# Adaptive weights accumulated in two 128x1024 operations per load in place of four of 128x512

## What is computed

```
cond = jax.nn.silu(c)
for i in range(DEPTH):
    mod = (cond @ ada_w[i] + ada_b[i])[:, None, :]
    sh1, sc1, gt1, sh2, sc2, gt2 = jnp.split(mod, N_MOD, axis=-1)
    h = rms_norm(x, norm1_w[i]) * (1 + sc1) + sh1
    ...                                   # the mixer gives y
    x = x + (1 + gt1) * y
    h = rms_norm(x, norm2_w[i]) * (1 + sc2) + sh2
    x = x + (1 + gt2) * swiglu_ffn(h, ffn_w1[i], ffn_w3[i], ffn_w2[i])
```

## Time and profile before

| | before |
|---|---|
| device time, three runs | 2332.69, 2333.07, 2337.92 us; median 2333.07 |
| profiled execution, its own time | 2324.39 us |
| its span (first to last instruction) | 2322.7 us |
| VectorE busy | 1470.6 us (63%) |
| of it adaptive operations (line 892) | 270.7 us, 384 operations |
| TensorE busy | 1992.9 us (86%) |
| ScalarE busy | 887.3 us (38%) |
| device memory read | 343.93 MB |

### The profile page before, as it was taken

One profiled execution on the slowest core, in us unless ns is written; L12 is line 12 of the kernel. 1 busy time (PEld: TensorE's weight loads), 2 busy tenths in 40 slices (PEclk: granted clock), 3 DMA queues, 4 the chain that ended last, 5 costly groups with the idle time before them and its releaser, 6 DMA issues.

```text
span 2322.7 us, 32348 instructions
## 1 busy us (share of the span) xinstructions
PE 1992.9 (86%) x13189; PEld 1746.3 (75%) x13189; DVE 1470.6 (63%) x2054; ACT 887.3 (38%) x1293; POOL 38.1 (2%) x61
## 2 busy tenths in 40 slices
PE   0597998699979988888898899996889888997998
PEld 0586786688758788883897689666887787886996
DVE  0599588688663666624788623346886497574553
ACT  1243753344332211102444434533443344664552
POOL 3000000100000000000000000001000000000000
PEclk9998999799979999959899889667999699998999
DMA  2554078399704200002698623024888152153562
GB/s 85 178 154 137 32 252 282 121 310 310 265 12 152 84 1 1 1 1 91 218 317 311 224 62 124 15 73 149 304 298 291 30 163 91 55 176 115 183 200 108
DMA packets 221029, 347.08 MB, mean 149 GB/s; under 512 B 12561, under 2 KB 178017, under 8 KB 220881
## 3 DMA queue, kind: packets, MB, share of 16 engines
q1 hardware_dynamic: 215024, 344.22, 44.5%
q10 hardware_dynamic: 5600, 0.36, 0.2%
q0 software_dynamic: 256, 0.43, 0.1%
HBM read 343.93 MB, written 1.05 MB: 149 GB/s over the span
## 4 chain that ended last, share of the span: by engine, by line
PE 48%; DVE 27%; DMA 12%; ACT 8%; issue 4%; ACTq 1%; DVEq 0%
PE psum_dve L353 19%; PE psum_act L353 16%; PE psum_acc L353 11%; DMA ring<-in_ffn_w_dram 9%; DVE arena L892 5%; DVE w_lo L922 5%; DVE arena L1039 4%; ACT w_hi L1348 3%; DMA dskip<-in_m_D_dram 2%; DVE arena L1036 1%; DVE arena L1232 1%; DVE arena L1202 1%; ACT arena L1420 1%; PE psum_act L356 1%; DVE arena L962 1%
## 5 line engine op out<-in xcount | busy, mean ns | idle before, releaser
L922 DVE TENSOR_TENSOR w_lo<-ring,w_hi 128x1024 fp32r<-128x1024 f32 x424 | 508.4, 1223 | 250.3 <-ACT w_hi L1348 247.5
L1348 ACT ACTIVATE w_hi<-ring 128x1024 fp32r<-128x1024 f32 x424 | 450.5, 1062 | 498.4 <-DMA ring<-in_ffn_w_dram 296.7
L353 PE MATMUL psum_dve<-h_lo,w_hi 128*128 128x256 f32 x1216 | 341.3, 281 | 0.0
L353 PE MATMUL psum_act<-h_lo,w_hi 128*128 128x256 f32 x1088 | 308.5, 284 | 0.0
L892 DVE SCALAR_TENSOR_TENSOR arena<-ring,vcol,arena 128x512 f32<-128x512 f32 x384 | 270.7, 748 | 11.1 <-DMA ring<-in_ada_w_dram 7.4
L353 PE MATMUL psum_dve<-arena 128*128 128x128 f32 (+5 forms) x1760 | 228.4, 318 | 16.0 <-DVE arena L1261 4.7
L353 PE MATMUL psum_act<-h_hi_ffn,w_hi 128*128 128x256 f32 x704 | 202.6, 288 | 35.4 <-DVE w_lo L922 18.3
L353 PEld LDWEIGHTS psum_dve<-h_lo,w_hi 128*128 128x128 f32 x1216 | 230.6, 190 | 0.0
L353 PEld LDWEIGHTS psum_dve<-arena 128*128 128x128 f32 (+3 forms) x1760 | 183.7, 193 | 46.3 <-issue 17.0
L353 PE MATMUL psum_dve<-h_hi_ffn,w_hi 128*128 128x256 f32 x704 | 198.0, 281 | 13.8 <-DVE w_lo L922 13.7
L353 PEld LDWEIGHTS psum_act<-h_lo,w_hi 128*128 128x128 f32 x1088 | 209.7, 193 | 0.1
(11 more groups left out here) (249 smaller groups left out, 3431.0 us busy)
## 6 DMA issues: line engine op xcount, KB each, us to landing
ring<-in_ffn_w_dram SPq DMA_DIRECT2D x132, 1024.0 KB, 5.5
ring<-in_ada_w_dram SPq DMA_DIRECT2D x96, 1024.0 KB, 5.4
ring<-in_m_in_w_dram SPq DMA_DIRECT2D x48, 1024.0 KB, 5.4
ring<-in_m_out_w_dram SPq DMA_DIRECT2D x16, 1024.0 KB, 5.6
ring<-in_r_w_rkv_dram SPq DMA_DIRECT2D x12, 1024.0 KB, 5.1
ring<-in_f_qkvf_w_dram SPq DMA_DIRECT2D x12, 1024.0 KB, 5.3
ring<-in_r_out_w_dram SPq DMA_DIRECT2D x4, 1024.0 KB, 4.9
ring<-in_f_out_w_dram SPq DMA_DIRECT2D x4, 1024.0 KB, 4.8
```

The costliest lines, as they stand in the source:

```text
L353: return nc.tensor.matmul(o, l, r, start=start, stop=stop, skip_group_check=True)
L922: tell(V.tensor_tensor(o, raw, hi, ALU.subtract), split_ready, hold=False)
L1348: tell(A(o, raw, ACT.Copy), hi_ready)
```

## The change

Each adaptive load is accumulated by two operations of 128x1024 (k = 0, then k = 1) instead of four of 128x512. The arithmetic for each element and its order (k = 0, then k = 1) stay as they were. The wait for the previous adaptive load's last operation moves from behind the first operation to ahead of it. The first operation is now held (VectorE waits for its completion, since the second adds to all that it wrote), the second is not, and releases the slot as before. No instruction changes its place with regard to others; loads, transfers and the other engines' instructions are the same.

```
-                for k in range(2):
-                    for hf in range(2):
-                        if (k, hf) == (0, 1) and counts.get("ada_slot_used"):
-                            dve.wait_ge(ada_used, counts["ada_slot_used"])
-                        o = ada[:, m * D + hf * NB:m * D + (hf + 1) * NB]
-                        ins = V.scalar_tensor_tensor(out=o, in0=slot(n)[:, k * D + hf * NB:k * D + (hf + 1) * NB],
-                                                     scalar=col("c", 2 * k4 + k), in1=o, op0=ALU.mult, op1=ALU.add)
-                        if k == 1 and hf == 1:
-                            tell(ins, ada_used, hold=False)
-                        else:
-                            counts["dve_step"] = counts.get("dve_step", 0) + 1
-                            ins.then_inc(dve_step, 1)
-                            dve.wait_ge(dve_step, counts["dve_step"] - (1 - k if hf == 0 else 1))
+                o = ada[:, m * D:(m + 1) * D]
+                if counts.get("ada_slot_used"):
+                    dve.wait_ge(ada_used, counts["ada_slot_used"])
+                for k in range(2):
+                    ins = V.scalar_tensor_tensor(out=o, in0=slot(n)[:, k * D:(k + 1) * D], scalar=col("c", 2 * k4 + k),
+                                                 in1=o, op0=ALU.mult, op1=ALU.add)
+                    tell(ins, ada_used, hold=False) if k else tell(ins)
```

## The result

The changed kernel takes 2344.42 us (median of 20 runs, 2332.63 to 2352.41), the kernel before 2333.52 us in 20 runs beside it (2300.33 to 2342.41). The ratio, formed over all runs, is 1.0080, with a 95% interval of 1.0052 to 1.0108; it is not the quotient of the two medians, which lie 10.9 us (0.5%) apart. The kernel became slower, not faster by 0.3%, and lies above the forecast range. How much slower is less sure: three of the 20 runs of before lie at 2300 to 2315 us and none of the changed kernel does. The means differ by 14.5 us with those three and by 10.4 us without them. The profiled execution took 2339.52 us, 15.1 us above that of before.

The account below looks back on a forecast made before the run. TensorE holds most of the chain, but up stretches turn on a loop of adaptive load, slot release and FFN transfer. 0.6 + 10.4 - 3.2 = 7.8 us gained: 2333.07 to 2325.3 us, range 2318 to 2333.5.

Parts of the forecast that it names:

- The operation and the waits: VectorE's adaptive loads: 1.28 us an operation, 2.51 instead of 2.77 us a load, 2.63 between neighbours at the start.
- the start: First eight adaptive loads, before TensorE begins at 75.96: 0.3 to 0.8 us sooner, taken as 0.6 us.
- my sum: At the start, five loads and the last bring 6 x 0.14 = 0.8 us; only first and last, 0.3.
- The loop and its 40 loads: Adaptive load, slot release, FFN transfer, split, mostly in up stretches: 40 loads on the chain save 0.26 each, 10.4 us.
- What is given back: FFN transfers asked for 0.26 us sooner behind the adaptive one take 0.10 us longer: 32 x 0.10 = 3.2 us lost.
- 32 turns: Of the 40 adaptive loads on the chain, some 32 are followed there by a transfer started 0.26 us sooner.
- my two ends: Bounds on a transfer's growth when asked for 0.26 us sooner: shallow 0.04 us, steep 0.44 us; 0.10 taken.
- Rival (c): Transfers grow 0.44 us on 32 turns: 3.4 us slower, 2336.5; from the 7.1 us landing alone, 2347. Chance 0.10.
- Rival (b): FFN load lands a fixed time behind the adaptive one, whenever asked for: 2.4 us gained, 2330.7. Chance 0.21.
- (a): Transfers keep their length: 11.2 us gained, 2321.9; 2318 with the operation at its low end. Chance 0.20.
- (d): The longer VectorE operation takes 1.49 instead of 1.28 us: 40 loads cost 7 us, 2340. Chance 0.02.

Follow-up runs that it names:

- the repeat: The changed kernel unaltered, measured again on another chip: 2335.40 us, ratio 1.0051 to the kernel before.
- the still pairs: Only pairs of an adaptive and an FFN load on an otherwise still core, no kernel work: 8.1 us to the second landing at 2.71 us spacing.
- the half loads: Adaptive loads bring 128 of 256 rows: 2303.14 us (0.9899) in the form of before, 2299.91 us (0.9883) in the changed form.
- the removed hold: Kernel before with one hold in each adaptive load taken out, its completion awaited ahead of the next adaptive load: 2324.25 us, ratio 1.0010.
- first pair: Four ring slots and four split buffers, first measurement of both forms: changed 2265.85 us (0.9747), form of before 2248.57 us (0.9708).
- first group of experiments: First four experiment kernels (copy between the operations, hold taken out, half-byte loads in both forms) on one chip; kernel before beside them 2322.4 us.
- the copy behind k = 1: Changed kernel with an extra held 128x128 copy behind each adaptive load's second operation, after the slot's release: 2333.89 us, ratio 1.0058.
- the three copies: Changed kernel with three held 128x128 copies between the two operations of each adaptive load: 2338.19 us, ratio 1.0066.

## Why the prediction was wrong

**The operation and the waits: right, but for the start.** 1282 ns against 1.28 us, 2.52 against 2.51 us a load, 246.2 us busy. At the start the chain reads (start, us):

```profile
52.92 1.30 DVE arena L891
...
55.63 1.30 DVE arena L891
...
63.69 5.95 DMA ring<-in_ada_w_dram
...
75.12 6.97 PE psum_dve L353 x32
```

Two neighbours stand 2.71 us apart, not 2.63. TensorE begins at 75.12 in place of 75.96, 0.84 us sooner, a little beyond the upper end of my 0.3 to 0.8 us, but not by my sum: the transfer on the chain kept its length, yet it is now the one behind the fourth load, with two loads behind it, where it was the one behind the fifth, with one. That the number fits is in part luck.

**The loop and its 40 loads: right as a mechanism.** The chain of the changed kernel turns through the same pieces, the adaptive operations on it fall from 126.3 to 117.0 us (9.3 us; the sum had 11.0 with the start), layer 3 kept its 112.0 us, and taking the transfer off the chain with a fourth slot emptied the up stretches down to TensorE's own time.

**"What is given back": the step that failed.** I let the transfer grow by 0.10 us for 0.26 us of spacing. Measured is 0.54 us as the mean of all FFN loads of the up stretches (5.91 to 6.45), 0.44 in the repeat (6.35), and 0.59 on the pairs that stand alone (5.80 to 6.39). On 32 turns 0.54 us is 17.3 us, and 11.0 - 17.3 is 6 us slower, where the medians show 10.9 and the two profiled executions 15.1. So this one term turns the sign; the rest is not accounted for by it. The chain shows where some of it is: the FFN transfers on it take 234.7 us in 37 pieces instead of 203.3 in 35, and those of the output projection 26.7 in four instead of 10.2 in two. So there are more transfers on the chain, beside longer ones, which a sum with a fixed count of 32 can't hold. That the bunching of the requests is the reason for these was not tried.

The fault was in how I bounded it. Of my two ends, 0.04 and 0.44 us, I took a value near the shallow one because most requests follow a gap of over 3 us, and the measured value lies at or beyond the steep one. That gap was the wrong one to look at: it is the one ahead of the adaptive load, and the one that shrank stands behind it. And I drew a straight line between landings at gaps of 7 us and of 3.4 us, when the time to the second landing does not follow the spacing in a line at all: in the kernels nothing is lost down to 2.63 us, and the loss is there at 2.51; in the still pairs it grows from 2.7 to 2.3. The change starts just beside that point. The rows that I had, 7.1 and 5.8 us at a spacing of 2.27, were on the far side of it.

**Rival (c)** is what happened: its place and its point of decision (0.26 us of stretch) hold, the result of 2344.4 us lies between its two prices of 2336.5 and 2347, and 0.10 was too little chance for it. I quoted the Trainium skill there ("DMA: Bandwidth & Descriptors", "Latency and other measured facts") for memory latency that rises under high load. The runs give it no support as the cause: the hump appears with two transfers on a still core, and at 3.0 us of spacing, where the same two still overlap, there is none of it. **Rival (b)** is what the half loads show, and what the removed hold agrees with: within limits the landing does not depend on when it was asked for, and VectorE's saving is worth next to nothing. **(a)** and **(d)** fell.

## What to carry to other kernels

Where a ring of buffers makes the end of one engine's step the request for the next transfer, a faster step is a change of the transfers' spacing, and its price is to be read there: count the landing from the request ahead of it, not from its own. Here a step that changed the spacing from 2.77 to 2.52 us cost more than it saved, and with a delay of 0.28 us on the queue that issues the landings and the stretches were again those of before. One more slot in the ring was worth some 60 us or more here, where the shorter step had promised 8: with it, landings of 6.8 us cost nothing.

## What the runs showed of the hardware

- A second 1 MiB transfer on the same queue can land later, in absolute time, the sooner it is asked for. With rows of 4 KiB first and of 1 KiB behind them, on a still core, it lands 9.2 to 8.9 us from the first request when asked for 2.0 to 2.4 us behind it, and 8.1 us at 2.7. With rows of 4 KiB in both it is 9.6 us at 2.0 and 8.0 at 2.75; with 1 KiB in both 8.9 at 1.75 and 8.3 at 2.75. The delay is in the last packets (8.87 against 7.62 us for the last, 6.23 against 5.99 for the median, at 1.97 and 2.71). A first load with rows of 4 KiB is not delayed (5.1 to 5.3 us). Why is open.
- A TensorE effect apart from the change makes the runs spread. In layer 2's attention the granted clock is a mix of 1.2 and 2.4 GHz; in the profiled execution of before its mean is 0.74 over 148.3 us, in the four-slot form of before (first pair) 0.90, and the same work takes 132.0 us:

```profile
1424.70:1573.00 148.30, 137.88 (x668) 103.69 (x667) 60.39 (x172) 62.68 (x151) 0.00 (x0) 0.74 0.18 57
```

```profile
1388.00:1520.00 132.00, 117.62 (x675) 92.37 (x673) 60.48 (x172) 62.44 (x151) 0.00 (x0) 0.90 0.19 60
```

  That is 16 us from one execution to another, more than the whole effect of the change; the runs of the four-slot form of before fall into two groups, 2244 to 2252 and 2267 to 2275 us. The times go with the clock: of the 24 runs of before in the first group of experiments, the eight with a mean granted clock of 0.925 or more took 2297.3 to 2314.5 us, the other sixteen 2317.3 to 2331.6. This is why the stretches and landings, and not the medians alone, carry the conclusions above. It does not explain the loss: a part of this attention (in the trace of before 1460.4 to 1567.4 us) takes 106.8 to 107.1 us at a mean of 0.65 in twelve of the fifteen traces of whole kernels, those of the kernel before, the changed one and its repeat among them; the exceptions are the copy behind k = 1 (104.6), the three copies (102.9) and this four-slot kernel (89.9). The work of VectorE and ScalarE in the two stretches shown is the same, and what decides the clock there was not tried.
